# Two-layer attention encoder on one core: output banks drained one step later, B's output blocks summed in pairs, dense work respread

## The chip, the cores and the metric

The kernel runs on one core of one Trainium2 chip, in one launch. The metric is the device time of that launch in microseconds. The engines are TensorE (PE; its weight loads PEld overlap its matmuls), VectorE (DVE), ScalarE (ACT), GpSimd (POOL) and SyncE (SP, which issues the DMAs). They run their own instruction streams and meet only at semaphores.

## What is computed

An encoder of two layers on x (1 × 1024 × 1024, float32). Each layer is a norm, an input projection, attention by heads, a gate and an output projection, then a norm and a residual sum. Layer 0 has two kinds of heads side by side: A, differential attention (4 heads, two softmaxes each, all earlier keys), and B, a sliding window (8 query heads, 2 heads of keys and values, one chunk of 64 back, with learned sinks). Layer 1 has C, 16 heads over a band of nine chunks with a learned relative bias.

```python
D_MODEL = 1024; SEQ = 1024; DEPTH = 2; CHUNK = 64; HEAD_DIM = 64
A_HEADS = 4; B_HEADS = 8; B_KV_HEADS = 2; B_PREV_CHUNKS = 1; C_HEADS = 16; C_PREV_CHUNKS = 8
# A, per head: two softmaxes
s = jnp.where(allowed, s - slopes[None, :, None, None, None] * dist, NEG)
p = jax.nn.softmax(s, axis=-1)
a = p[:, :, 0] - lam * p[:, :, 1]
o = rms_norm(einsum('bhqk,bkhe->bqhe', a, v), subln_g) * (1.0 - lam_init)
# B, per head: band of two chunks, a sink in the softmax
p = jax.nn.softmax(jnp.concatenate([s, sink], axis=-1), axis=-1)[..., :-1]
# C, per head: band of nine chunks, learned bias
p = jax.nn.softmax(jnp.where(valid, q @ k * scale + bias, NEG), axis=-1)
# each layer: every branch times its gate g * sigmoid(g), output projection, then
x = x + rms_norm(concat(branches * silu(gates)) @ w_out, post_norm_g)
```

## The kernel before, in words

**Precision.** Every float32 operand of a product is split into a rounded part and a rest (hi and lo, type fp32r), and each product is three matmuls: hi·hi, hi·lo, lo·hi. The weights are split by POOL (`split`, L799 and L802), everything else by ACT (hi) and DVE (lo).

**Tiling.** A tile is 128 rows or columns. A unit is two heads (A: one head with its two softmaxes): A0 to A3, B0 to B7 (each half of the sequence of a pair of heads), C0 to C7. A unit of A or C has 16 items, one for each tile of 128 queries of a head, in 20 steps; a B unit has 8 items in 8 steps. Units start at steps 0, 20, 40, 60 (A), 80 to 136 by 8 (B), then 8 steps of bridge between the layers, C0 at 152, C1 at 172 and so on; 322 steps in all.

**The steps.** A planner in Python lays the whole program out in steps. Each engine walks the steps in the same order, and its stream is fixed by the code of that walk:

- PE in step s: an early use of the output bank (only when the step has two or more), the input products of the step (`project`, L926, 128×512 each, 24 to a fill of a bank), a late use of the output bank, product of the probabilities with v (`times_v`, L1004), transposes of probabilities (`turn`, L1048), scores (`score`, L1078), then further late uses, the last outputs and transposes of v.
- ACT: the hi part of transposed probabilities (L1205), exp (L1176), the hi parts of fills, and so on.
- DVE in iteration s: `lo_of_turned` (L1474) and `lowest` (L1410: scores plus bias and their minimum) of step s−1; `normalise` (L1420, L1424; for A also L1429, L1432) of step s−2, for the units that are not deferred (A and C1 to C6); `denominators` (L1449) of step s−2 for the deferred ones (B, C0, C7), which are normalised after the product with v by `times_rec` (L1458); the gate; the lo parts of fills; and the uses of the output bank of step s; `out_sum` (L1482).

**Banks.** Input fills go to dense banks 0 and 1 in turn. All uses of the output bank, number 2, are called spare uses: output products (three matmuls L933 for one head pair, 128 rows and 512 columns, that DVE adds into y: L1387, for A L1379 and L1381 with the norm's factor, for C0 a copy L1385), row transposes of the norm between the layers (L960), and A's sums of squares (L954). PE may write the bank again when DVE has read it (`bank_free[2]`). Output products of unit i run during unit i+1: for A and C one use per step in 16 of the steps 3 to 19. B's run two per step in steps 13 to 16 from the start of their unit; A3's in steps 3 to 8 of B0, C6's in steps 3 to 8 of C7.

**lowest** of step s−1 waits for the semaphore `scored`, which the last scores matmul of the step raises, and PE's later scores wait for `lowest` in turn (`low_done`).

Of the kernel before, what the change touches and what calls it, by code (L numbers as in the profile page):

```python
# [13 lines left out]
P = 128  # L14
# [25 lines left out]
class Unit:  # L40
# [35 lines left out]

    def order(self):
# [13 lines left out]
C = [Unit("C", i, 80 + 64 + BRIDGE + 20 * i) for i in range(8)]  # L91
# [3 lines left out]
TOTAL = C[7].start + 30  # L95
# [59 lines left out]
class Fill:  # L155
# [7 lines left out]
    hi: int = 0  # L163


@dataclass(eq=False)
class Spare:
# [3 lines left out]
    u: Unit = None  # L171
    row: int = 0
    half: int = 0
    block: object = None
# [24 lines left out]
for u_ in UNITS:  # L199
    for j_, (h_, t_) in enumerate(u_.order()):  # L200
        k0_ = {"A": 0, "B": max(0, t_ - 1), "C": max(0, t_ - 4)}[u_.kind]
        it_ = Item(u_, h_, t_, len(ITEMS), u_.start + j_, k0_, t_ + 1 - k0_)
# [18 lines left out]
        if u_.kind != "A" or h_ == 1:  # L221
            g_ = Turned("p", u_, -1, it_.step + 3, item=it_, first=ITEMS[-2] if u_.kind == "A" else it_)
            GROUPS.append(g_)
            it_.group = len(GROUPS) - 1
            if t_ % 2:
                pv_ = Pv(u_, h_, t_ - 1, len(PVS), g_.step + 1, g_)
# [23 lines left out]
V_TURNS += [Turned("v", C[i], 6 + i, C[i - 1].start + 19) for i in range(1, 8)]  # L250
# [56 lines left out]
for i_ in range(8):  # L307
    f_ = B[i_].half
    segment([("g", B[i_], f_)] + ([("q", B[i_ + 1], B[i_ + 1].half)] if i_ < 7 else []), B[i_].start, B[i_].start + 7)
segment([("q", C[0], 0), ("k", C[0], 0), ("v", C[0], 0), ("g", C[0], 0)], C[0].start - BRIDGE, C[0].start - 1)  # L310
segment([("q", C[0], 1), ("k", C[0], 1)], C[0].start + 8, C[0].start + 8)
segment([("v", C[0], 1)], C[0].start + 9, C[0].start + 10)
segment([("g", C[0], 1)] + both("v", C[1]), C[0].start + 11, C[0].start + 15)
for i_ in range(7):
    if i_:
        segment(both("g", C[i_]) + both("v", C[i_ + 1]), C[i_].start, C[i_].start + 15)
    if i_ < 6:
        segment(both("k", C[i_ + 1]) + both("q", C[i_ + 1]), C[i_].start + 16, C[i_].start + 19)
segment([("k", C[7], 0), ("q", C[7], 0)], C[6].start + 16, C[6].start + 19)
segment([("k", C[7], 1), ("q", C[7], 1), ("g", C[7], 0), ("g", C[7], 1)], C[7].start, C[7].start + 7)  # L320
# [1328 lines left out]
```

## Time and profile before

| | us |
|---|---|
| median of 3 runs (lowest, highest) | 1391.14 (1386.51, 1396.16) |
| the profiled execution | 1392.36 |
| its span, from first to last instruction | 1390.4 |
| PE busy in it | 1234.1 (89%) |
| DVE busy | 891.2 (64%) |
| ACT busy | 580.6 (42%) |
| POOL busy | 389.3 (28%) |

The mean granted TensorE clock of the profiled execution was 0.952 of full speed. The steps stand in the trace at: A1 to A3 131 to 358 us, B0 to B4 358 to 520, B5 to B7 520 to 638, bridge 638 to 675, C0 675 to 800, C1 to C6 800 to 1260, C7 and the end from 1260 on. A busy time counts the instructions of an engine on one clock; matmuls overlap each other in the records, so the distance of two starts is the time that a matmul takes from PE, not its recorded length. "A <- B" in the waits is an idle time of A that ended when B finished.

### The profile page before, as it was taken

To read this page: it belongs to the slowest core of one execution; us is meant where nothing else is said; L and a number is where in the kernel's file an instruction comes from. 1 tells how busy PE (TensorE), PEld (TensorE's weight loads), DVE (VectorE), ACT (ScalarE), POOL (GpSimd) and SP (SyncE) were. 2 spreads that over 40 slices of the span, in tenths; PEclk is the share of its full clock that TensorE was granted. 3 is DMA by queue.
4 is the path that set the end of the run, shared out by engine and by line. 5 is a ranking of instruction groups with operands and counts; after the bars stand their busy time and mean duration, and the time that the engine had idled before them with its cause. 6 is when DMAs were issued, how large, how long until landed. Compare 5 with 4: busy or idle time off the path is not lost.

```text
span 1390.4 us, 17337 instructions
## 1 busy us (share of the span) xinstructions
PE 1234.1 (89%) x6480; PEld 1043.0 (75%) x6480; DVE 891.2 (64%) x1789; ACT 580.6 (42%) x1271; POOL 389.3 (28%) x280
## 2 busy tenths in 40 slices
PE   6999999999878877768568999999999999998863
PEld 6978888888766665656457888888888888886652
DVE  5575857677576676765444386766847586675667
ACT  5544434434333434433333444444444354443332
POOL 4322131231423334433722212213230222312002
PEclk9999999999999999889779999999999999999976
DMA  6341020110211122222211111102110211111302
GB/s 197 107 127 61 16 62 16 35 42 16 62 46 46 48 78 91 91 76 61 91 61 46 51 46 50 46 16 65 31 65 16 65 31 50 46 35 31 121 31 91
DMA packets 86243, 82.07 MB, mean 59 GB/s; under 512 B 3184, under 2 KB 74864, under 8 KB 86160
## 3 DMA queue, kind: packets, MB, share of 16 engines
q1 hardware_dynamic: 86160, 80.97, 18.6%
q8 instruction: 51, 0.84, 0.3%
q14 instruction: 32, 0.26, 0.1%
HBM read 72.52 MB, written 13.68 MB: 62 GB/s over the span
## 4 chain that ended last, share of the span: by engine, by line
PE 74%; DVE 13%; ACT 5%; issue 4%; POOL 2%; DMA 1%; SPq 0%; POOLq 0%; DVEq 0%; ACTq 0%
PE dense L926 38%; PE dense L933 13%; PE pv_ps L1004 8%; PE scores L1078 6%; PE turned L1048 5%; PE dense L901 3%; DVE e_sb L1410 2%; DVE y L1387 2%; DVE rec_wide L1449 1%; DVE pT_lo L1474 1%; ACT e_sb L1176 1%; DVE yT_lo L1530 1%; PE dense L960 1%; ACT pT_hi L1205 1%; PE turned L1036 1%
## 5 line engine op out<-in xcount | busy, mean ns | idle before, releaser
L926 PE MATMUL dense<-hT_hi,w_hi 128*128 128x512 f32 x880 | 354.8, 403 | 0.0
L926 PE MATMUL dense<-hT_lo,w_hi 128*128 128x512 f32 x880 | 348.5, 396 | 0.0
L926 PE MATMUL dense<-hT_hi,w_lo 128*128 128x512 f32 x880 | 347.9, 395 | 0.0
L1176 ACT ACTIVATE e_sb<-e_sb,low 128x256 f32<-128x256 f32 (+7 forms) x256 | 170.7, 667 | 371.3 <-DVE low L1410 371.3
L799 POOL TENSOR_SCALAR w_hi<-w_f 128x1024 fp32r<-128x1024 f32 x90 | 102.0, 1133 | 793.2 <-PE dense L926 663.7
L802 POOL TENSOR_TENSOR w_lo<-w_f,w_hi 128x1024 fp32r<-128x1024 f32 x90 | 219.7, 2441 | 7.5
L926 PEld LDWEIGHTS dense<-hT_hi,w_lo 128*128 128x128 f32 x880 | 167.8, 191 | 37.7
L926 PEld LDWEIGHTS dense<-hT_lo,w_hi 128*128 128x128 f32 x880 | 168.6, 192 | 28.9
L926 PEld LDWEIGHTS dense<-hT_hi,w_hi 128*128 128x128 f32 x880 | 168.4, 191 | 29.2
L1474 DVE TENSOR_TENSOR pT_lo<-turned,pT_hi 128x640 fp32r<-128x640 f32 (+3 forms) x224 | 133.7, 597 | 55.7 <-ACT pT_hi L1205 52.7
L933 PE MATMUL dense<-w_hi,yT_hi 128*128 128x512 f32 x256 | 111.0, 434 | 62.6 <-DVE y L1387 43.6
L1004 PE MATMUL pv_ps<-pT_hi,v_st 128*128 128x256 f32 x536 | 133.3, 296 | 27.6 <-DVE pT_lo L1474 27.6
L1387 DVE TENSOR_TENSOR y<-dense,y 128x512 f32<-128x512 f32 x160 | 110.1, 688 | 64.3 <-PE dense L933 63.1
L1205 ACT ACTIVATE pT_hi<-turned 128x640 fp32r<-128x640 f32 (+3 forms) x224 | 117.1, 523 | 63.1 <-PE turned L1048 60.7
L1078 PE MATMUL scores<-k_hh,q_st 128*128 128x384 f32 (+3 forms) x352 | 130.4, 370 | 4.9 <-DVE k_l L1357 3.5
L1410 DVE CUSTOM_DVE_ANT_0 e_sb<-scores,bias 128x640 f32<-128x640 f32 (+3 forms) x192 | 130.9, 682 | 4.2 <-PE scores L1078 2.8
L1048 PE MATMUL turned<-ident,e_sb 128*128 128x128 f32 x744 | 121.8, 279 | 8.0 <-DVE pT_lo L1474 6.5
L1004 PEld LDWEIGHTS pv_ps<-pT_hi,v_st 128*128 128x128 f32 x536 | 101.5, 198 | 36.0 <-DVE pT_lo L1474 32.3
L1004 PE MATMUL pv_ps<-pT_lo,v_st 128*128 128x256 f32 x456 | 122.2, 292 | 0.0
L933 PEld LDWEIGHTS dense<-w_hi,yT_hi 128*128 128x128 f32 x256 | 50.5, 197 | 91.0 <-DVE y L1387 56.3
L1048 PEld LDWEIGHTS turned<-ident,e_sb 128*128 128x128 f32 x744 | 93.6, 143 | 25.3 <-DVE pT_lo L1474 7.4
L1078 PE MATMUL scores<-k_l,q_st 128*128 128x384 f32 (+3 forms) x352 | 111.4, 325 | 0.0
(128 smaller groups left out, 1789.5 us busy)
## 6 DMA issues: line engine op xcount, KB each, us to landing
w_f<-in_w_in_c SPq DMA_DIRECT2D x36, 512.0 KB, 4.0
w_f<-in_w_in_ab SPq DMA_DIRECT2D x34, 512.0 KB, 3.9
w_f<-in_w_out_ab SPq DMA_DIRECT2D x12, 512.0 KB, 3.6
rel_tiles_dram<-rel_rows_dram SPq DMA_DIRECT2D x1, 5120.0 KB, 23.1
bias<-rel_tiles_dram SPq DMA_DIRECT2D x8, 640.0 KB, 5.3
y<-in_x SPq DMA_DIRECT2D x8, 512.0 KB, 7.7
xs<-in_x SPq DMA_DIRECT2D x8, 512.0 KB, 3.6
x_dram<-y SPq DMA_DIRECT2D x8, 512.0 KB, 4.1
```

The source lines that it names most:

```text
L799: ts(hi, src, 1.0, 1.0, ALU.mult, ALU.mult).then_inc(w_hi_done, 1)
L802: tt(w_lo[:, slot, :], src, hi, ALU.subtract).then_inc(w_ready, 1)
L926: last = mm(dense[:, x.n % 2, :], lhs[:, d * P:(d + 1) * P], rhs[:, d, x.f * HALF:(x.f + 1) * HALF], start=i == 0, stop=i == 23)
L933: last = mm(bank, lhs[:, cols], rhs, start=n == 0, stop=n == 2)
L1004: last = mm(pv_ps[:, p.n % 2, :], v_st[:, which, kt, :], p_part[:, kt - p.t + 6, :], start=i == 0 and m == 0, stop=i == p.count - 1 and m ...
L1048: last = nc.tensor.transpose(turned[:, at0:at0 + P], e_sb[:, e0:e0 + P], ident[:])
L1078: last = mm(scores[:, at0:at0 + w], q_st[:, it.h, c:c + P], k_part[:, kh, key:key + w], start=i == 0, stop=i == 1)
L1176: copy(e, e, ACT.Exp, scale=-1.0, bias=stat_col(low, it.j), accum_out=stat_col(total, it.j)).then_inc(s_exp, 1)
L1205: copy(pT_hi[:, r, q], turned_tile(x), ACT.Copy).then_inc(s_thi, 1)
L1387: last = tt(into, dense[:, 2, :], into, ALU.add)
L1410: nc.vector.tensor_tensor_reduce(out=e_of(it), in0=scores[:, it.off:it.off + it.n * P], in1=bias_of(it), scale=-u.slope(it.h), scalar=star ...
L1474: tt(pT_lo[:, r, q], turned_tile(x), pT_hi[:, r, q], ALU.subtract).then_inc(s_tlo, 1)
```

## The change

1. **DVE drains the output bank an iteration later.** The uses of step s are read in iteration s+1 (all but an early one), and in an iteration `lowest` now comes first, then `lo_of_turned`, `normalise`, `denominators`, and only then the bank. Fills are drained one iteration later too, except in the last four steps of a unit of A or C (at the end of the same iteration). `out_sum`, `times_rec` and ACT's `out_low` move one step later. Further late uses behind the scores are gone from PE's step.
2. **B's outputs in pairs.** `out_matmuls` sums the blocks of two units B in one bank (six matmuls, one add into y instead of two). The weights of the second block need a place of their own, in vT (hi) and in the space of C's bias (lo, with a fourth and fifth load slot). The uses are spread, one per step, over steps 3 to 12 of the unit behind the pair and the next; A3's over steps 3 to 13 of B0 (one and two in turn).
3. **A narrow reciprocal.** The reciprocal of the deferred units is taken of four columns on DVE and widened to 128×256 by an ACT copy (`widen`), where it was taken of 128×256 on DVE.
4. **Deferred units turn their probabilities one step earlier** (two steps behind the scores), and for B there is a second set of columns of pT.
5. **Dense work is respread**: C0's later items one step later, C1 and all behind it one step later; the q of C0 is projected in B7, the v of C1 and C7 partly in steps 0 to 5 of C0 and C7, C7's k, q and g over its steps 0 to 9; C6's outputs are one per step over 16 steps of C7; the last outputs use two banks and come a step earlier. The program has 320 steps.

```diff
         for s in range(TOTAL):
+            for it in ITEMS_AT.get(s - 1, []):
+                lowest(it)
             for x in TURNED_AT[s - 1]:
                 lo_of_turned(x)
-            for it in ITEMS_AT.get(s - 1, []):
-                lowest(it)
             for it in ITEMS_AT.get(s - 2, []):
                 if not it.u.deferred:
                     normalise(it)
-            for r, it, _ in recs_at(s, 2):
+            for r, it in DENOMINATORS_AT[s]:
                 denominators(r, it)
...
+            for x in LATE_AT.get(s - 1, []) + EARLY_AT[s]:
+                spare_use(x)
+            for _, n, row, half, _ in LAST_AT.get(s - 1, []):
+                last_out(n, row, half)
+            for x in FILLS_AT[s]:
+                if not x.tail:
+                    lo_of_fill(x)
             for g in GATES_AT[s]:
                 gated(g)
+            for p in PVS_AT.get(s - 1, []):
+                out_sum(p)
+            for r, p in RECS_AT[s - 1]:
+                times_rec(r, p)
             for g in GATES_AT.get(s - 1, []):
                 gated_lo(g)
-            uses = SPARES_AT.get(s, [])
-            early = uses[:-1][:1]
-            for x in early:
-                spare_use(x)
...
-            for x in uses[len(early):]:
-                spare_use(x)
-            for _, n, row, half, _ in LAST_AT[s]:
-                last_out(n, row, half)
-            for p in PVS_AT[s]:
-                out_sum(p)
-            for r, it, p in recs_at(s, 5):
-                times_rec(r, it, p)
```

The pairs, their plan, the reciprocal and its copy:

```diff
-        def out_matmuls(bank, cols, w, w_l):
-            for n, (lhs, rhs) in enumerate(((yT_hi, w), (yT_hi, w_l), (yT_lo, w))):
-                last = mm(bank, lhs[:, cols], rhs, start=n == 0, stop=n == 2)
+        def out_matmuls(bank, parts):
+            for m, (c, w, w_l) in enumerate(parts):
+                for n, (lhs, rhs) in enumerate(((yT_hi, w), (yT_hi, w_l), (yT_lo, w))):
+                    last = mm(bank, lhs[:, c:c + P], rhs, start=m == n == 0, stop=m == len(parts) - 1 and n == 2)
...
-b0_ = B[0].start
-out_steps(A[3], [(b0_ + 3, 3), (b0_ + 4, 3), (b0_ + 5, 3), (b0_ + 6, 3), (b0_ + 7, 2), (b0_ + 8, 2)])
-for i_ in range(7):
-    s_ = B[i_].start + 13
-    out_steps(B[i_], [(s_, 2), (s_ + 1, 2), (s_ + 2, 2), (s_ + 3, 2)])
+out_steps((A[3],), [(B[0].start + 3 + t, 1 + t % 2) for t in range(11)])
+for i_ in range(0, 6, 2):
+    s_ = B[i_ + 1].start + 8
+    out_steps((B[i_], B[i_ + 1]), [(s_ + t, 1) for t in (3, 4, 6, 7, 8, 9, 11, 12)])
...
-out_steps(C[6], [(s_ + 3, 3), (s_ + 4, 3), (s_ + 5, 3), (s_ + 6, 3), (s_ + 7, 2), (s_ + 8, 2)])
+out_steps((C[6],), [(s_ + 4 + t, 1) for t in range(16)], (2, 3, 4, 5, 6, 7, 0, 1))
...
-            nc.vector.reciprocal(rec_wide[:].rearrange("p (o h a) -> p h o a", o=2, h=2),
-                                 src.rearrange("p (h o a) -> p h o a", h=2, a=1).broadcast_to([P, 2, 2, HD])).then_inc(s_drec, 1)
+            nc.vector.reciprocal(stat_col(rec, it.j - 3, 4), src).then_inc(s_drec, 1)
```

DVE in a step of C before, in a unit that is not deferred: `pT_lo` is the lo part of the transposed probabilities, the ISA rows are `lowest`, `y` the add of the output bank.

```order
L1474 TENSOR_TENSOR pT_lo<-turned,pT_hi 128x5x128 [waits turned_hi]
L1410 ISA e_sb,low<-scores,bias 128x640 [waits turned_done,scored]
L1410 ISA low 128x1
L1420 RECIPROCAL rec<-total 128x1 [waits exp_done]
L1424 TENSOR_SCALAR e_sb<-e_sb,rec 128x640 [waits rec_done]
L1387 TENSOR_TENSOR y<-dense,y 128x512 [waits spare_filled]
L1482 TENSOR_TENSOR o_sb<-pv_ps,o_sb 64x256 [waits pv_low]
```

And in the same step after:

```order
L1485 ISA e_sb,low<-scores,bias 128x640 [waits turned_done,scored]
L1485 ISA low 128x1
L1546 TENSOR_TENSOR pT_lo<-turned,pT_hi 128x5x128 [waits turned_hi]
L1495 RECIPROCAL rec<-total 128x1 [waits exp_done]
L1499 TENSOR_SCALAR e_sb<-e_sb,rec 128x640 [waits rec_done]
L1462 TENSOR_TENSOR y<-dense,y 128x512 [waits spare_filled]
L1554 TENSOR_TENSOR o_sb<-pv_ps,o_sb 64x256 [waits pv_low]
```

The two ISA rows have moved ahead of `pT_lo`. The y add stands at the same distance from them as before, but it is now that of the step whose scores these ISA rows wait for; before it was that of the next step.

PE in the same step after (its rows are in the same order before), L992 being the input products, L1000 the output products:

```order
L992 MATMUL dense<-hT_lo,w_hi 128x512
L992 MATMUL dense<-hT_hi,w_lo 128x512
L1000 MATMUL dense<-w_hi,yT_hi 128x512 [waits bank_free2]
L1000 MATMUL dense<-w_lo,yT_hi 128x512
L1000 MATMUL dense<-w_hi,yT_lo 128x512
L1111 MATMUL turned<-ident,e_sb 128x128 [waits probs,turned_lo]
L1111 MATMUL turned<-ident,e_sb 128x128 x4
L1141 MATMUL scores<-k_hh,q_st 128x384 [waits low_done]
L1141 MATMUL scores<-k_l_57,q_st 128x384
L1141 MATMUL scores<-k_hh,q_st 128x256
```

The output products wait for `bank_free2`, which the y add raises, behind the input products of their step.

DVE in B before, where output products stand two to a step and the wide reciprocal is at its place:

```order
L1410 ISA e_sb,low<-scores,bias_b,sinks 128x256 [waits turned_done,scored]
L1410 ISA low 128x1
L1387 TENSOR_TENSOR y<-dense,y 128x512 [waits spare_filled] x2
L1458 TENSOR_TENSOR o_sb<-o_sb,pv_ps 128x256 [waits out_bc,rec_turned]
L1474 TENSOR_TENSOR pT_lo<-turned,pT_hi 128x2x128 [waits turned_hi]
L1410 ISA e_sb,low<-scores,bias_b,sinks 128x128 [waits turned_done,scored]
L1410 ISA low 128x1
L1443 TENSOR_TENSOR den<-total,sink_e 128x4 [waits sink_e,exp_done]
L1449 RECIPROCAL rec_wide<-den 128x2x2x64 [waits den_pair]
L1524 SCALAR_TENSOR_TENSOR o_sb<-o_sb,gate 128x256 [waits bank_free1,rec_times]
```

And after:

```order
L1485 ISA e_sb,low<-scores,bias_b,sinks 128x128 [waits turned_done,scored]
L1485 ISA low 128x1
L1546 TENSOR_TENSOR pT_lo<-turned,pT_hi 128x2x128 [waits turned_hi]
L1518 TENSOR_TENSOR den<-total,sink_e 128x4 [waits sink_e,exp_done]
L1522 RECIPROCAL rec<-den 128x4 [waits den_pair]
L1462 TENSOR_TENSOR y<-dense,y 128x512 [waits spare_filled]
L1596 SCALAR_TENSOR_TENSOR o_sb<-o_sb,gate 128x256 [waits bank_free1,rec_times]
L1485 ISA e_sb,low<-scores,bias_b,sinks 128x256 [waits turned_done,scored]
L1485 ISA low 128x1
```

One y add stands where two did, and the reciprocal has four columns.

## Rows read from the trace of the kernel before

**Rows 1.** The page: its head and section 1
```profile
span 1390.4 us, 17337 instructions
...
PE 1234.1 (89%) x6480; PEld 1043.0 (75%) x6480; DVE 891.2 (64%) x1789; ACT 580.6 (42%) x1271; POOL 389.3 (28%) x280
```

**Rows 2.** Windows: from:to and length (us), busy (x instructions), PEclk, DMA share, GB/s
```profile
131.00:358.00 227.00, 226.89 (x1197) 193.56 (x1197) 160.79 (x304) 96.90 (x187) 57.72 (x32) 1.00 0.13 40
358.00:520.00 162.00, 131.26 (x658) 105.80 (x657) 110.13 (x239) 60.06 (x179) 53.55 (x35) 0.97 0.17 50
520.00:638.00 118.00, 87.03 (x400) 68.53 (x399) 77.16 (x159) 47.68 (x131) 44.45 (x38) 0.86 0.25 77
638.00:675.00 37.00, 32.08 (x153) 25.81 (x152) 18.78 (x34) 11.75 (x26) 21.11 (x15) 1.00 0.28 79
675.00:718.00 43.00, 18.92 (x74) 14.55 (x73) 22.60 (x40) 17.30 (x41) 21.85 (x19) 0.61 0.28 90
718.00:800.00 82.00, 77.46 (x403) 66.23 (x402) 32.21 (x54) 31.02 (x58) 23.00 (x16) 0.96 0.16 48
800.00:1260.00 460.00, 459.79 (x2520) 396.73 (x2519) 311.65 (x699) 210.70 (x438) 100.05 (x68) 1.00 0.14 43
1260.00:1390.40 130.40, 85.41 (x388) 68.82 (x386) 81.86 (x132) 41.71 (x87) 21.01 (x21) 0.83 0.18 69
```

**Rows 3.** Waits in 358:638: who, for whom: us in total, times, longest
```profile
PE dense L933 <- DVE y L1387: 31.6, 23, 3.6
```

**Rows 4.** Timeline, a step of C1: start us, us, engine, line, operation
```profile
915.74 0.28 PE L1078 MATMUL scores<-k_l,q_st 128*128 128x256 f32 x1
...
915.85 0.40 PE L926 MATMUL dense<-hT_hi,w_hi 128*128 128x512 f32 x1
...
916.20 0.82 DVE L1474 TENSOR_TENSOR pT_lo<-turned,pT_hi 128x640 fp32r<-128x640 f32 x1 [0.38 <-ACT pT_hi L1205]
...
916.94 0.82 DVE L1410 CUSTOM_DVE_ANT_0 e_sb<-scores,bias 128x640 f32<-128x640 f32 x1
...
917.22 0.39 PE L933 MATMUL dense<-w_hi,yT_hi 128*128 128x512 f32 x1
...
917.68 0.16 DVE L1420 RECIPROCAL rec<-total 128x1 f32<-128x1 f32 x1
...
917.88 0.56 DVE L1424 TENSOR_SCALAR e_sb<-e_sb,rec 128x640 f32<-128x640 f32 x1
...
918.35 0.68 DVE L1387 TENSOR_TENSOR y<-dense,y 128x512 f32<-128x512 f32 x1
```

**Rows 5.** Timeline, DVE in a step of A2
```profile
245.82 1.08 DVE L1410 CUSTOM_DVE_ANT_0 e_sb<-scores,bias 128x896 f32<-128x896 f32 x1
...
247.02 0.68 DVE L1429 TENSOR_SCALAR e_sb<-e_sb,rec,neg_lam 128x768 f32<-128x768 f32 x1
247.74 1.02 DVE L1432 SCALAR_TENSOR_TENSOR e_sb<-e_sb,rec 128x768 f32<-128x768 f32 x1
248.67 0.75 DVE L1381 SCALAR_TENSOR_TENSOR y<-dense,rms,y 128x512 f32<-128x512 f32 x1
```

**Rows 6.** Timeline, PE's wait for the y add in a B step
```profile
511.30 0.68 DVE L1387 TENSOR_TENSOR y<-dense,y 128x512 f32<-128x512 f32 x1
...
512.04 0.50 PE L933 MATMUL dense<-w_hi,yT_hi 128*128 128x512 f32 x1 [0.48 <-DVE y L1387]
...
512.38 0.40 PE L933 MATMUL dense<-w_lo,yT_hi 128*128 128x512 f32 x1
```

**Rows 7.** Lines by form, DVE in 358:638: group | busy us, mean ns | idle before
```profile
L1449 DVE RECIPROCAL rec_wide<-den 128x256 f32<-128x256 f32 x15 | 26.3, 1753 | 0.5
L1410 DVE CUSTOM_DVE_ANT_0 e_sb<-scores,bias_b,sinks 128x256 f32<-128x256 f32 x55 | 26.1, 475 | 0.2 <-PE scores L1078 0.2
L1474 DVE TENSOR_TENSOR pT_lo<-turned,pT_hi 128x256 fp32r<-128x256 f32 x52 | 21.9, 421 | 9.6 <-ACT pT_hi L1205 9.0
```

**Rows 8.** Lines by form, DVE in 131:358
```profile
L1432 DVE SCALAR_TENSOR_TENSOR e_sb<-e_sb,rec 128x896 f32<-128x896 f32 x3 | 9.5, 3174 | 0.1
```

More of the change, by code:

```diff
@@ L75, in place, with step, in_tail @@
         return slice(f * HALF, (f + 1) * HALF)
+    def step(self, j):
+        return self.start + j + (1 if self.kind == "C" and self.i == 0 and j >= 8 else 0)
+    def in_tail(self, s):
+        return self.kind != "B" and s >= self.step(16)
     def order(self):
@@ L94 @@
     u_.n = n_
[L95 removed]
+TOTAL = C[7].start + 27
 @dataclass(eq=False)
@@ L163 @@
     hi: int = 0
+    tail: bool = False
+    drain: int = 0
 @dataclass(eq=False)
@@ L170 @@
     use: int
-    u: Unit = None
+    units: tuple = ()
     row: int = 0
     half: int = 0
-    block: object = None
+    blocks: tuple = ()
 @dataclass(eq=False)
@@ L326, with out_steps @@
     f_.hi = sum(1 for o_ in FILLS[:f_.n] if o_.b != "v")
+    f_.tail = any(u_.in_tail(f_.step) and f_.step < u_.step(20) for u_ in UNITS if u_ is not C[7])
+    f_.drain = f_.step if f_.tail else f_.step + 1
 FILL_OF = {(f_.b, f_.u, f_.f): f_ for f_ in FILLS}
 SPARE_RAW = []
-def out_steps(u, plan):
-    rows = range(4 * u.half, 4 * u.half + 4) if u.kind == "B" else range(ST)
+def out_steps(units, plan, rows=None):
+    if rows is None:
+        rows = range(4 * units[0].half, 4 * units[0].half + 4) if units[0].kind == "B" else range(ST)
     fills = [(row, half) for row in rows for half in range(2)]
@@ L338, in out_steps @@
         for row, half in fills[n:n + count]:
-            SPARE_RAW.append((step, "out", u, row, half))
+            SPARE_RAW.append((step, "out", units, row, half))
         n += count
-    assert n == len(fills), (u, n)
+    assert n == len(fills), (units, n)
 def even_plan(first, n, steps):
@@ L430, in freed @@
             return ("pro", PRO_DONE[b], 0)
+    if blocks[n].u is B[1]:
+        return ("spare", SUM_OF[A[3]].use + 1, B[0].start + 1)
+    if blocks[n].u is B[7]:
+        return ("fill", FILL_OF["g", B[7], 1].n + 1, FILL_OF["g", B[7], 1].step)
     return None
@@ L479, in final_rows, with gate_of @@
     return [(n, row) for a, n, row in FINAL if a + lag == s]
+def gate_of(u, row):
+    c = u.col(row)
+    return max(g.n for g in GATES if g.u is u and same_columns(g.cols, slice(c, c + P)))
 def previous_gate(u, cols):
@@ L747, in _ @@
             for w in LOADS_AT.get(s, []):
+                if w.u is B[1] and w.b == "o":
+                    if new(s_low, 64):
+                        sp.wait_ge(s_low, 64)
                 freed_by(w.slot_free)
```

284 lines of the change are left out of this document (160 added, 124 removed).

## The prediction

> **What bounds the kernel now.** I read the page's head first, then the table of windows, because the head mixes stages with different limits. PE is busy for 1234.1 of 1390.4 us and DVE for 891.2 [rows 1]. By windows there are two kinds of stage [rows 2]. In A1 to A3 (131 to 358) and C1 to C6 (800 to 1260) PE is busy for 226.89 of 227 us and for 459.79 of 460 at clock 1.00: there its own matmuls set the time, half of the kernel. In B0 to B7 and the bridge (358 to 675) it is busy for 131.3 + 87.0 + 32.1 = 250.4 of 317 us, and the clock falls to 0.97 and 0.86. At the entry of layer 1 (675 to 718) and in the tail (1260 on) it waits too. In B the largest waits of PE are for the output bank: 31.6 us in 23 waits for the y add L1387 [rows 3].
>
> **Where the new loop is.** All output products use one bank, and the y add on DVE frees it. Before, DVE adds the use of step s in iteration s, ahead of anything that needs the scores of s. After, it adds the use of step s in iteration s+1, behind lowest(s), which waits for the last matmul of step s; lo_of_turned(s), the reciprocal and normalise stand ahead of it too. PE reaches the output products of s+1 after only the six input products. So from the last scores of step s two paths run to the next output products, and the longer one sets the time.
>
> PE's own path: the six input products take from 915.85 to 917.22, 1.37 us or 0.23 each [rows 4].
> DVE's path, for a C step of five key tiles [rows 4]: the last scores matmul is issued at 915.74 and runs 0.28, so it ends 0.17 after PE's next issue at 915.85; lowest takes 0.74 (916.94 to 917.68), lo_of_turned 0.74 (916.20 to 916.94), reciprocal 0.20 (917.68 to 917.88), normalise 0.47 (917.88 to 918.35), the add 0.68. For the end of the add to PE's restart, a wait in B shows 511.30 + 0.68 = 511.98 to 512.04, and 0.34 instead of 0.23 to the next product [rows 6]: 0.06 + 0.11. With 0.02 to DVE's start that is 0.36 + 0.74 + 0.74 + 0.20 + 0.47 + 0.68 = 3.19 us, so PE waits 3.19 − 1.37 = **1.82 us in every such step**.
>
> **C1 to C6.** The first output use has nothing to wait for. Then each unit has one step of about 0.64 (less normalising), and the steps up to 15 sum to 17.3 us with the shorter tiles of the first rows; 0.5 is added for DVE instructions slowed while POOL writes. The last four steps have 24 input products, 24 × 0.23 = 5.5 us, ahead of the output products and hide it all. That gives 17.8 us per unit, 89 for C1 to C5. C6 has only 4.5 products of cover per step (36 over 16 steps less; 12 waits × 1.5 × 0.23 = 4.1 more) and loses 24 products to C7 (5.4): 17.8 + 4.1 − 6 (rounded with one out use gone) = 16. **C: +105.** Reordering lo and lowest by itself costs nothing: PE waits for neither by the rows.
>
> **A1 to A3.** The chain is longer. At 7 tiles lowest is 1.08 against 0.82 at 5 [rows 4, 5], at 6 tiles the two normalise instructions take 0.72 and 0.93 (247.02 to 248.67), the add 0.75 [rows 5]. Per tile I take 0.13 for lowest and, alike, for lo_of_turned, and 0.2 for the pair (an estimate from these). Odd steps (a turned group and two normalised heads) wait 1.49 to 3.82, mean 2.65, six of them: 15.9; even steps have no lo_of_turned and wait 0.30 to 0.96: 3.8. Where POOL is splitting weights the second normalise takes 3174 ns at 896 columns [rows 8] against 1.02 us at 768 [rows 5]: about 2.3 per unit reaches the loop now that DVE is on PE's path. 22 us per unit. **A: +66.**
>
> **B and the bridge.** The pairs put two heads' blocks in one bank: 32 fewer adds of 0.69 on DVE (22 us), the products of PE stay. The wide reciprocal, 1753 ns [rows 7], becomes one of four columns (0.16, as the reciprocal of one column in rows 4) and a copy on ACT, which is busy for 108 of 280 us there [rows 2]: 15 × 1.6 = 24 us of DVE freed in B. DVE was busy for 187 of 280, so PE no longer waits for it to catch up. The same loop bounds what is gained, without normalise: 0.36 + 0.40 (lowest, 0.475 less overlap) + 0.34 (lo_of_turned, 0.421 likewise) + 0.69 = 1.79 against 1.37, 0.42 per step, 3.4 per unit of eight steps. PE's work by the pitch of its matmuls (0.23, 0.12 and 0.11) is 22.5 to 25 per unit. B0 to B4 become 137 (from 162), B5 to B7, where row norms and a lower clock add 16, become 100 (from 118) and the bridge 32 (from 37). **B: −48.** Bounds: all waits for L1387 stay but for the adds saved (−20); all of 66.6 idle and the clock loss of some 21 come back, and A3's outs spread well (−100 with the bridge at its work).
>
> **Entry of layer 1.** A step of C0 is put in, but a fill of C0's q is made in B7 already, and 718 to 800 loses 6 us of products that stand elsewhere now (its v of C1 in the first steps, where PE is busy for 18.9 of 43). The chain of 675 to 718, whose clock is 0.61, stays. **−7**, bounds 0 and −15.
>
> **Tail.** PE is busy for 85.4 and DVE for 81.9 of 130.4. Four wide reciprocals less 1.6 each, the last outputs a step earlier and the 24 products of C6 (+5.4, in idle time) against the C6 outputs spread one per step: **−16**, bounds 0 and −35.
>
> **Other edits.** Waits of the additional weight slots and the later loads of C's bias fall on SP and POOL, whose splits wait for PE in most cases; I take them as free (if a split came late a fill would wait a few us; that lies in the range). The ACT reordering puts exp ahead of the fills, with ACT at 43 to 46% in A and C: nothing.
>
> **Sum** against the profiled execution's own 1392.4 (span 1390.4 and 2.0 around it): + 66 + 105 − 48 − 7 − 16 = 1492. The profiled one stands 1.2 above the median, so **1491 us**.
>
> A rule that speaks against the change. The trace shows one output bank that cost nothing in A and C, 0.2 us of 460 [rows 2], as long as its add came early. The Trainium skill (Perfetto Trace Analysis, Optimizing Tensor Performance (Matmuls)) wants independent matmul groups to rotate through different PSUM banks so that the evacuation of one overlaps the next group. By that rule alone only the add itself would be exposed, 0.68 us in 12 steps of 9 units, 73 us, where the rows give 171: what is queued ahead of the evacuation counts for more than the evacuation.
>
> **The rivals.**
> 1. *The loop and the clock as well* (0.14). In B0 to B4, where PE is idle for 19% of the time in short waits, the granted clock was 0.97, and 0.86 in B5 to B7 at 26% [rows 2]. A and C would be idle for 19 to 22%, in waits of under 4 us. At 0.97 over the 860 us of these stages as they become that is +26: 1517. Against it: the waits are short, with 3 to 6 us of full work between.
> The Trainium skill (TensorE: Matmul & The Clock Gate, A second HAM failure mode: psum-queue depth-cycling) describes just such micro-idling between matmul groups that makes the clock oscillate; no row of before in A or C shows it.
> 2. *A smaller loop* (0.10). If PE's end, the restart and the collisions overlap, A and C cost 133 instead of 171, and B and the tail may give 15 more: about 1440.
> 3. *A wash* (0.04): the loop at its lower bound, 133, and the gains near their upper ones, 133 of 100 + 15 + 35: 1391.
> 4. *Faster* (0.04): the add is hidden in A and C after all, because DVE reaches it inside PE's cover. It decides where the chain is under 1.37 us; the add and lowest alone are 1.42, so it needs DVE not to wait for the step's last scores. Then only the gains are left: 1391 − 71 = 1320. For it speaks that DVE is busy for only 68% of 800 to 1260.
> The forecast itself has 0.68.
>
> **The numbers.** The forecast's own range is 1455 to 1525 (the loop 150 to 193 with the gains between 50 and 90); rival 1 lies in it. With rival 2's edge the range is **1440 to 1530**, some 0.82. What a measurement of this kernel can tell from no change is about 1%. Faster by over 1%: 0.05 (rival 4 and part of 3); within 1%: 0.03; slower: 0.92.
>
> **What would show it.** In the profile after: waits of PE's output products L1000 for the y adds L1462 of about 1.8 us in nearly every step of C1 to C6, some 12 per unit, and PE's busy share of 100% down to about 80%; a C unit of 96 us (78.5 before), an A unit of 98 (76 before). DVE idle ahead of lowest L1485 for PE's scores, where now it comes to scores that are long done. The 15 wide reciprocals of B gone, a B unit of 26 us for 31. The clock at 1.00 in A and C (rival 1: under 0.98). I am wrong if A1 to A3 and C1 to C6 keep their 227 and 460 us, or if those waits stay under 1 us.

## The result, and the profile after

The changed kernel takes 1547.38 us, median of 4 runs (1544.52 to 1549.66), against 1390.82 for the kernel before measured beside it: 1.112 times as long, 95% interval 1.108 to 1.117. The forecast was 1491 with a range to 1530: the direction was right, the size too small by 56 us, a third of the slowdown of 157.

The profiled execution has a span of 1542.6 us. Its page, head and section 1, in the form of [rows 1]:

```profile
span 1542.6 us, 17427 instructions
...
PE 1275.5 (83%) x6480; PEld 1045.7 (68%) x6480; DVE 830.5 (54%) x1758; ACT 588.6 (38%) x1296; POOL 395.5 (26%) x286
```

DVE does 61 us less than before and waits more. PE has the same 6480 matmuls and is busy for 41 us more: some of them ran at half clock, and the record of the first matmul behind a wait is longer (C1 has no half clock, and PE is busy for 81.8 us in it against 78.9 without the waits, in the run with the add in its own step everywhere). The windows over the stages, to be read beside [rows 2] (A1 to A3; B0 to the bridge; the entry of layer 1 with the rest of C0; C1 to C6; the tail; columns as there):

```profile
129.30:442.20 312.90, 256.92 (x1204) 208.95 (x1202) 162.40 (x304) 96.00 (x187) 58.25 (x33) 0.91 0.10 29
442.20:715.70 273.50, 234.42 (x1194) 188.56 (x1192) 160.09 (x399) 127.22 (x353) 119.51 (x89) 0.96 0.24 74
715.70:847.60 131.90, 98.64 (x485) 81.35 (x485) 48.12 (x93) 47.66 (x101) 45.64 (x36) 0.87 0.19 61
847.60:1424.20 576.60, 483.53 (x2496) 393.92 (x2493) 309.18 (x698) 211.04 (x437) 100.87 (x70) 0.98 0.11 35
1424.20:1542.60 118.40, 88.42 (x410) 72.84 (x408) 75.45 (x133) 43.74 (x93) 23.88 (x23) 0.84 0.21 80
```

| stage | before, us | after, us | difference | forecast |
|---|---|---|---|---|
| ahead of A1 | 131.0 | 129.3 | −2 | 0 |
| A1 to A3 | 227 | 312.9 | +86 | +66 |
| B0 to the bridge | 317 | 273.5 | −43 | −48 |
| C0 | 125 | 131.9 | +7 | −7 |
| C1 to C6 | 460 | 576.6 | +117 | +105 |
| tail | 130.4 | 118.4 | −12 | −16 |

In the two stages that were PE's own, PE is now busy for 82% and 84%. DVE and ACT do the same work in them as before; they only wait longer. The waits of the stretch of C1 to C6 (who, for whom: us in total, times, longest):

```profile
DVE e_sb L1485 <- PE scores L1141: 169.9, 78, 5.2
...
PE dense L1000 <- DVE y L1462: 74.0, 61, 2.1
...
PE dense L1000 <- DVE y L1460: 14.3, 12, 2.1
...
PE dense L1000 <- DVE yT_lo L1602: 4.7, 6, 1.9
```

The first and the second row are the two halves of a loop: DVE waits for PE's scores, then PE waits for DVE's add. 73 waits for the two forms of the add stand in the trace, and six, one per unit, for the lo part of the gated output (L1602). Their mean is 1.2 us, less than the 1.82 of the forecast, since steps with shorter tiles wait less and a row counts 0.28 us less than the wait costs (shown with a step below).

### The profile page after: what moved, and what is told of

The parts are those of the page before. It is cut to its first block, busy times and chain, and to the rows that moved or that the text cites. A ratio compares the mean times of both kernels' runs of the same rounds, so it can differ in the third digit from the quotient of the medians.

```text
span 1542.6 us, 17427 instructions
## 1 busy us (share of the span) xinstructions
PE 1275.5 (83%) x6480; PEld 1045.7 (68%) x6480; DVE 830.5 (54%) x1758; ACT 588.6 (38%) x1296; POOL 395.5 (26%) x286
## 4 chain that ended last, share of the span: by engine, by line
PE 58%; DVE 27%; issue 3%; ACT 3%; POOL 1%; DMA 1%; DVEq 0%; POOLq 0%; ACTq 0%
PE dense L992 22%; PE dense L1000 14%; PE pv_ps L1067 8%; PE scores L1141 6%; DVE e_sb L1485 6%; PE turned L1111 5%; DVE pT_lo L1546 5%; DVE y L1462 3%; DVE e_sb L1499 3%; DVE e_sb L1507 2%; DVE y L1456 1%; DVE e_sb L1504 1%; DVE q_st L1425 1%; PE dense L1026 1%; PE turned L1099 1%
## 5 line engine op out<-in xcount | busy, mean ns | idle before, releaser
L992 PE MATMUL dense<-hT_hi,w_hi 128*128 128x512 f32 x880 | 357.1, 406 | 7.3 <-DVE k_l L1431 4.4
L992 PE MATMUL dense<-hT_lo,w_hi 128*128 128x512 f32 x880 | 349.8, 397 | 0.0
L992 PE MATMUL dense<-hT_hi,w_lo 128*128 128x512 f32 x880 | 349.3, 397 | 0.0
L864 POOL TENSOR_SCALAR w_hi<-w_f 128x1024 fp32r<-128x1024 f32 x88 | 96.6, 1098 | 955.9 <-PE dense L992 846.2
L1000 PE MATMUL dense<-w_hi,yT_hi 128*128 128x512 f32 x224 | 109.1, 487 | 187.5 <-DVE y L1462 93.1
L1000 PEld LDWEIGHTS dense<-w_hi,yT_hi 128*128 128x128 f32 x224 | 43.5, 194 | 256.3 <-DVE y L1462 131.3
L867 POOL TENSOR_TENSOR w_lo<-w_f,w_hi 128x1024 fp32r<-128x1024 f32 x88 | 215.0, 2443 | 7.3
L992 PEld LDWEIGHTS dense<-hT_hi,w_hi 128*128 128x128 f32 x880 | 169.6, 193 | 36.1 <-issue 8.2
L992 PEld LDWEIGHTS dense<-hT_hi,w_lo 128*128 128x128 f32 x880 | 168.6, 192 | 37.6
L992 PEld LDWEIGHTS dense<-hT_lo,w_hi 128*128 128x128 f32 x880 | 169.8, 193 | 27.2
L1067 PE MATMUL pv_ps<-pT_hi,v_st 128*128 128x256 f32 x536 | 141.7, 310 | 3.5 <-DVE pT_lo L1546 2.9
L1067 PE MATMUL pv_ps<-pT_lo,v_st 128*128 128x256 f32 x456 | 126.5, 301 | 0.0
L1067 PEld LDWEIGHTS pv_ps<-pT_hi,v_st 128*128 128x128 f32 x536 | 109.1, 214 | 10.0 <-DVE pT_lo L1546 5.1
L1111 PEld LDWEIGHTS turned<-ident,e_sb 128*128 128x128 f32 x744 | 94.2, 144 | 20.2 <-DVE pT_lo L1546 1.9
L1067 PEld LDWEIGHTS pv_ps<-pT_lo,v_st 128*128 128x128 f32 x456 | 96.0, 211 | 4.0
```

Source lines behind the costliest of these rows:

```text
L864: ts(hi, src, 1.0, 1.0, ALU.mult, ALU.mult).then_inc(w_hi_done, 1)
L867: tt(lo_place(slot), src, hi, ALU.subtract).then_inc(w_ready, 1)
L992: last = mm(dense[:, x.n % 2, :], lhs[:, d * P:(d + 1) * P], rhs[:, d, x.f * HALF:(x.f + 1) * HALF], start=i == 0, stop=i == 23)
L1000: last = mm(bank, lhs[:, c:c + P], rhs, start=m == n == 0, stop=m == len(parts) - 1 and n == 2)
L1067: last = mm(pv_ps[:, p.n % 2, :], v_st[:, which, kt, :], p_part[:, kt - p.t + 6 - pT_set(p), :], start=i == 0 and m == 0, stop=i == p.coun ...
L1111: last = nc.tensor.transpose(turned[:, at0:at0 + P], e_sb[:, e0:e0 + P], ident[:])
```

## The experiments

Each run is compared with the kernel before on the same chip; the stages are cut in each trace at the first products of their first step, 1.4 to 4.2 us ahead of its first scores. Stages and waits are those of the profiled execution, times and ratios those of the medians.

### The add made in its own step again, in A and C alone

```diff
+OWN = set(range(A[1].start, A[3].start + 20)) | set(range(C[1].start, C[7].start))
+DRAIN_AT = {s: ([] if s - 1 in OWN else LATE_AT.get(s - 1, [])) + EARLY_AT[s] + (LATE_AT[s] if s in OWN else []) for s in range(TOTAL)}
...
-            for x in LATE_AT.get(s - 1, []) + EARLY_AT[s]:
+            for x in DRAIN_AT[s]:
                 spare_use(x)
```

> The changed kernel, in which DVE again adds the output bank's use of step s in iteration s (at the same place of the iteration) in A1 to A3 and C1 to C6 alone; everything else stays, lowest ahead of lo_of_turned too. If the late add is the loop that costs the time, A1 to A3 fall from 312.9 us back to about 227 and C1 to C6 from 576.6 to about 455 (24 products fewer than before), PE is busy for over 99% there at clock 1.00, and the time is about 1547 - 86 - 121 = 1340 us. If the time went into something else of the change (lowest ahead of lo_of_turned, fills and out_sum read a step later, the turned groups), these stages keep most of their length and the time stays above 1500.

It took 1351.44 us (1350.42 to 1352.86), 0.970 of the kernel before (0.967 to 0.973), 196 us less than the changed kernel. The windows of A1 to A3 and of C1 to C6:

```profile
130.80:363.40 232.60, 229.44 (x1203) 193.55 (x1201) 159.57 (x304) 94.42 (x187) 59.22 (x33) 1.00 0.13 39
...
769.60:1234.40 464.80, 458.51 (x2494) 391.78 (x2493) 314.63 (x698) 211.35 (x438) 102.54 (x69) 1.00 0.14 43
```

80 and 112 us are back, PE is busy for 98.6% at clock 1.00. What is left over 227 and 455 is 6 and 10 us; an experiment below takes 3 of it, and the rest stays open. So the place of one DVE instruction per step is worth 192 us here, and without it the rest of the change is a gain of 3%.

### The same in every step

The edit is the one above with OWN set to all steps; ACT's part of the row transposes moves along.

> The same edit in every step of the program, B, C0 and C7 as well (ACT's part of the row transposes moves along). If the loop costs B about 0.4 us in each of its steps with an output, and C0's row transposes go through the same bank, it is 10 to 25 us below the run that edits A and C alone: 1315 to 1330. If B, C0 and C7 are held by other things (the chain through exp, denominators and the gate), it is within 5 us of that run; if DVE now waits for PE's later output products and holds up its chain, it is above it.

1335.18 us (1331.29 to 1336.82), 0.958 of before (0.955 to 0.961). B with the bridge goes from 272.6 to 268.0 us, the first eight steps of C0 from 50.4 to 42.7. PE's waits in those eight steps, of the run above and then of this one:

```profile
PE dense L1028 <- DVE hT_lo L1441: 13.7, 4, 8.2
...
PE dense L1028 <- DVE xs L1676: 8.0, 2, 6.7
```

```profile
PE dense L1028 <- DVE xs L1676: 8.3, 3, 4.1
...
PE dense L1028 <- DVE hT_lo L1441: 3.4, 2, 1.9
```

The row transposes use the output bank as well, and DVE's `hT_lo` frees it: the loop stood there too, 8.2 us long at its worst, since ahead of the second read stood what waits for the scores.

### The late add kept, PE's output products behind its scores

```diff
+            if s not in OWN:
+                for x in LATE_AT[s]:
+                    spare_use(x)
...
                 score(it)
+            if s in OWN:
+                for x in LATE_AT[s]:
+                    spare_use(x)
```

> The changed kernel with DVE's late add kept, but in A1 to A3 and C1 to C6 PE makes the output products of a step behind its scores instead of behind its input products. The add of step s-1 then has a whole PE step of cover (2.6 to 5 us) instead of the six input products' 1.37. If it is the short cover that makes the loop, A1 to A3 and C1 to C6 are back at about 227 and 455 us and the time is 1340, as with the early add. If the late add is bad by itself (DVE busier, or its clock effects), the time stays well above that.

1368.51 us (1367.78 to 1371.38), 0.983 of before (0.980 to 0.986). C1 to C6 take 464 us, as with the early add: a whole step covers a chain of 3.2 us, late add or not. A1 to A3 take 248, 15 more than with the early add, so 1340 was too low. PE still waits for the y add there, 15.7 us in twelve waits, four in each unit (0.9, 1.6, 2.0 and up to 1.1 us). They stand in the later steps of the unit, where DVE's chain is longest. It is the cover against the chain that decides, in both directions.

### The late add alone, in the kernel before

```diff
                 denominators(r, it)
             if s == 1:
                 constants()
+            if s - 1 in OWN:
+                for x in SPARES_AT.get(s - 1, []):
+                    spare_use(x)
...
             early = uses[:-1][:1]
+            if s in OWN:
+                uses, early = [], []
```

> The kernel before with one part of the change: in A1 to A3 and C1 to C6 the add of step s's output bank is made in iteration s+1, behind lo_of_turned, lowest, normalise and denominators. Nothing of B, C0 and C7 is touched. If this alone makes the loop, A1 to A3 take about 313 us instead of 227 and C1 to C6 about 575 instead of 460, and the time is about 1391 + 86 + 113 = 1590 us, slower than the whole change. If the loop needs the other parts as well, it stays below 1450.

1597.13 us (1593.85 to 1601.78), 1.147 of before (1.143 to 1.151). Windows of A1 to A3 and C1 to C6:

```profile
128.80:441.80 313.00, 257.65 (x1204) 210.78 (x1202) 161.84 (x304) 97.36 (x187) 58.27 (x34) 0.91 0.10 29
888.00:1467.50 579.50, 486.68 (x2524) 396.96 (x2521) 308.59 (x700) 211.47 (x438) 99.73 (x69) 0.99 0.11 34
```

The stages are those of the whole change within 3 us (C6 has its 24 products more here). The late add is enough by itself; no other part of the change is needed for the loop.

### The late add directly behind lowest

```diff
                 lowest(it)
+            if s - 1 in OWN:
+                for x in LATE_AT[s - 1]:
+                    spare_use(x)
             for x in TURNED_AT[s - 1]:
                 lo_of_turned(x)
```

> The changed kernel with the late add kept (step s in iteration s+1) in A1 to A3 and C1 to C6, but directly behind lowest, so that lo_of_turned, the reciprocal and normalise no longer stand ahead of it. By the sum of the chain a C step of five tiles waits 0.36 + 0.74 + 0.68 - 1.37 = 0.41 us instead of 1.85, an A step of n tiles 0.13n - 0.18 instead of up to 3.8, and the clock has no cause left to fall in A. That is 250 us for A1 to A3 (312.9), 491 for C1 to C6 (576.6) and a time of about 1398. If the time of the loop is not the sum of what stands ahead of the add, but a fixed cost of waiting for the scores, it stays above 1480.

1400.22 us (1395.8 to 1404.14, 10 runs), 1.005 of before (1.004 to 1.007). Windows of A1 to A3 and C1 to C6:

```profile
129.50:385.60 256.10, 237.55 (x1204) 192.93 (x1202) 164.81 (x304) 95.99 (x187) 55.83 (x33) 0.99 0.12 36
787.50:1275.60 488.10, 472.12 (x2496) 384.68 (x2493) 311.15 (x698) 211.16 (x437) 101.34 (x70) 1.00 0.13 41
```

That is 256 and 488, against 250 and 491 from the sum of the chain. The add still waits for the step's last scores, yet 147 us are back: the wait is the sum of what stands between the scores and the add, and lo_of_turned, the reciprocal and normalise were most of it.

### lo_of_turned ahead of lowest again, late add kept

```diff
+            for x in TURNED_AT[s - 1]:
+                lo_of_turned(x)
             for it in ITEMS_AT.get(s - 1, []):
                 lowest(it)
-            for x in TURNED_AT[s - 1]:
-                lo_of_turned(x)
```

> The changed kernel with the old order of two DVE operations alone: lo_of_turned ahead of lowest again, the late add kept. lo_of_turned needs only the transposes, which PE makes ahead of the scores, and takes 0.74 us at 5 tiles. If all that stands ahead of the add counts wherever it stands, the loop keeps its length and the time stays at 1547 within 10 us. If what counts is only the part of the chain behind the scores, lo_of_turned partly runs while PE makes the scores (0.6 us at 5 tiles), the wait of 1.85 us shrinks by 0.3 to 0.6 in each step with a turned group, and the time is 1500 to 1530.

1573.2 us (1571.74 to 1575.78), 1.130 of before (1.127 to 1.133): 26 us slower than the changed kernel, outside both expectations. In A nothing moves (313), in C1 to C6 5 us. B and the bridge take 290 us against 273.5, 17 of the 31 between the two profiled executions. DVE's waits for ACT in B and the bridge, of the changed kernel and then of this one:

```profile
DVE pT_lo L1546 <- ACT pT_hi L1265: 3.4, 5, 0.9
```

```profile
DVE pT_lo L1546 <- ACT pT_hi L1265: 74.8, 40, 3.3
```

`lo_of_turned` waits for ACT's hi part, which ends later than the scores in B. With it first, lowest stands behind ACT's copy, and exp behind lowest. With lowest first, ACT's copy is hidden behind it. DVE's waits for the scores there fall from 63.1 to 1.2 us in return, so DVE itself waits only some 10 us more; but ACT's waits for `lowest`, ahead of exp, rise from 39.0 to 72.3 us. So this half of the reordering is a gain in B, which the prediction had put at nothing. That exp carries it to PE is argued from the order, not tested. In C the loop keeps its length for the same reason: in a step of C1 the hi part ends at 903.33 in the changed kernel, 0.15 us behind the last scores, so lo_of_turned can't run while PE makes the scores, as the second expectation had it.

### PE's waits in A filled with matmuls on zeros

```diff
+WAIT_FILL = {5: 4, 7: 8, 9: 8, 11: 10, 12: 2, 13: 12, 15: 21}
...
+                for _ in range(WAIT_FILL[j]):
+                    mm(dense[:, f.n % 2, :], zeros[:], hT_hi[:, 0, 0:HALF], start=False, stop=False)
```

> The changed kernel with PE's waits in A1 to A3 filled: in the steps where PE waits for the y add it makes 4 to 21 more matmuls of 128x512 whose stationary tile is zero (they add nothing to the bank), 2 to 21 of them per step, 0.9 to 4.8 us, a little less than each measured wait (1.2 to 5.5 us). PE then does not sit idle. The granted clock was 0.87 in A1's steps with waits (129 to 206), and matmuls behind the long waits stood 0.43 us apart instead of 0.23. If the rest of A's miss, some 9 us per unit over the forecast, is the clock that falls in the waits, A1 to A3 fall from 312.9 us to about 288 at clock 1.00 and the time to about 1522 us. If the clock's fall hides inside the waits and the miss is chain length, nothing comes back: 1547 or some us more.

1523.0 us (1521.06 to 1524.85), 1.093 of before (1.091 to 1.096): 195 more matmuls, and 24 us less than the changed kernel. The stretch of A1 to A3 is 293 us long, at clock 1.00:

```profile
129.30:422.00 292.70, 282.04 (x1406) 229.34 (x1404) 154.56 (x304) 96.06 (x187) 58.07 (x34) 1.00 0.11 32
```

A1 to A3 end 20.2 us earlier than in the changed kernel: 293 is the stage's length with the loop and a full clock, and the other 20 us were the clock. The changed kernel's trace shows how. PE in step 15 of A1 (the wait for the add, then the products with v), and windows of the same stretch:

```profile
194.36 0.39 PE L992 MATMUL dense<-hT_hi,w_lo 128*128 128x512 f32 x1
200.25 0.80 PE L1000 MATMUL dense<-w_hi,yT_hi 128*128 128x512 f32 x1 [5.49 <-DVE y L1454]
200.84 0.63 PE L1000 MATMUL dense<-w_lo,yT_hi 128*128 128x512 f32 x1
201.27 0.63 PE L1000 MATMUL dense<-w_hi,yT_lo 128*128 128x512 f32 x1
```

```profile
194.00:196.00 2.00, 0.75 (x4) 0.29 (x2) 1.96 (x5) 1.24 (x2) 1.07 (x2) 1.00 0.03 9
196.00:198.00 2.00, 0.00 (x0) 0.00 (x0) 1.97 (x2) 0.00 (x0) 2.00 (x1) 0.71 0.87 248
198.00:200.00 2.00, 0.00 (x0) 0.00 (x0) 2.00 (x2) 0.00 (x0) 0.58 (x1) 0.50 0.02 5
200.00:202.00 2.00, 1.75 (x5) 1.47 (x6) 0.19 (x1) 0.00 (x0) 0.00 (x0) 0.50 0.00 0
```

While PE stands still the granted clock falls from 1.00 to 0.50 (2.4 to 1.2 GHz), in the window from 196 to 198, and it is still there when the wait is over: products of 512 columns follow each other every 0.43 us (200.84 to 201.27) instead of 0.23. A wait need not be that long. In A1 to A3 the rows show fifteen waits of 2.1 us or more, and the clock fell to 0.50 in or within 1 us behind thirteen of them. In C1 to C6, where most waits are shorter and the longest is 2.1, it fell six times, each time behind a wait of 1.9 to 2.1 us, and others of that length left it alone. C1 has no such fall and C2 has one:

```profile
847.60:944.30 96.70, 81.78 (x431) 66.68 (x429) 52.26 (x118) 36.01 (x74) 18.02 (x13) 1.00 0.13 41
944.30:1042.50 98.20, 83.30 (x431) 68.28 (x430) 52.04 (x118) 35.81 (x74) 18.09 (x13) 0.98 0.11 34
```

C2 is 1.5 us longer with the same work, and C3, again without a fall, takes 96.7 us. At 1.5 us each the six falls cost C1 to C6 some 9 us (an estimate from these units; no run fills C's waits).

### The wide reciprocal put back, and the pairs undone

Both start from the kernel with the add in its own step everywhere (1335).

```diff
-            nc.vector.reciprocal(stat_col(rec, it.j - 3, 4), src).then_inc(s_drec, 1)
+            if new(s_rturn, r):
+                dve.wait_ge(s_rturn, r)
+            nc.vector.reciprocal(rec_wide[:].rearrange("p (o h a) -> p h o a", o=2, h=2),
+                                 src.rearrange("p (h o a) -> p h o a", h=2, a=1).broadcast_to([P, 2, 2, HD])).then_inc(s_drec, 1)
```

> Against the run with the early add in every step (1335): the wide reciprocal on DVE is put back (128x256, 1.75 us, no copy on ACT), all else kept. If DVE's 1.6 us more stand on a path to PE in B, C0 and C7 (24 of them), B grows from 268 us by 10 to 20 and the time is 1348 to 1362. If the reciprocal lay beside PE's work, the time stays at 1335 and the gain in B comes from the pairs and the spread.

1349.47 us (1349.03 to 1350.19): 14.3 us more, 12 of them in B and the bridge (279.9 against 268.0). DVE was freed of 24 × 1.6 = 38 us by it, so a good third of that reached the time. (ACT loses its copy of 0.41 us in return.)

```diff
         for row, half in fills[n:n + count]:
-            SPARE_RAW.append((step, "out", units, row, half))
+            for u in units:
+                SPARE_RAW.append((step, "out", (u,), row, half))
```

> Against the run with the early add in every step (1335): B's blocks are no longer summed in pairs in the bank; each of the two is a use of its own with its own add of 0.69 us, 32 adds more on DVE, in the same steps, PE's products unchanged. If the adds of DVE bound B, it is 10 to 25 us slower: 1345 to 1360. If DVE has room for them now that the reciprocal is narrow, the time is within 5 us of 1335.

1357.16 us (1353.95 to 1360.95): 22 us more, with 32 adds of 0.69 us more on DVE, 19 of them in B and the bridge. Here each added microsecond of DVE cost one of the kernel. The range of both: 0.969 (0.966 to 0.971) and 0.974 (0.971 to 0.978) of before.

### Two more waits taken away

```diff
-    f_.tail = any(u_.in_tail(f_.step) and f_.step < u_.step(20) for u_ in UNITS if u_ is not C[7])
+    f_.tail = f_.b in "kq" or any(u_.in_tail(f_.step) and f_.step < u_.step(20) for u_ in UNITS if u_ is not C[7])
...
+            for g in GATES_AT[s]:
+                if whole(g):
+                    gated(g)
+            for g in GATES_AT.get(s - 1, []):
+                if whole(g):
+                    gated_lo(g)
             for x in DRAIN_AT[s]:
                 spare_use(x)
```

> The run with the early add in every step, with two more waits of its trace taken away: k and q fills are read by ACT and DVE at the end of their own iteration (they were read one later, and the first scores of each B unit waited 2.3 to 2.9 us for q), and the whole-unit gates of A and C1 to C6 are computed ahead of the bank's adds (the first output product of 9 units waited 1.0 us for them). If these waits are ended by what the trace names, 7 x 2.4 + 9 x 0.9 = 25 us come back: 1310 us. If something else comes last there (exp, the v fills), less than 10 us come back.

1312.73 us (1311.28 to 1313.69), 0.942 of before (0.940 to 0.944), 22 us below the run that it starts from. B and the bridge fall from 268.0 to 255.5:

```profile
360.70:616.20 255.50, 227.65 (x1196) 188.26 (x1194) 160.66 (x399) 125.57 (x352) 119.40 (x89) 0.97 0.25 78
```

C0's second part falls from 82.9 to 74.2: PE no longer waits for `k_l` there, and the clock is 1.00 where it was 0.94, which takes the other 4.3 us off PE's busy time. The wait in the run that it starts from, in 673 to 756:

```profile
PE dense L994 <- DVE k_l L1433: 4.4, 1, 4.4
```

A1 to A3 gain 3 us, the earlier gates' part; C1 to C6 gain nothing (464.7), so there the first output product is held by something that comes last with the gate and that these runs don't name. This kernel beats both: it is 80 us below the kernel before, measured beside it.

Two further steps from it brought nothing. lo_of_turned ahead of lowest:

> The run with early add, own-iteration k and q fills and earlier gates (1313), with lo_of_turned ahead of lowest again. In its trace PE's product with v waits 0.5 us for pT_lo in 2 to 3 steps of each unit of A and C, since lowest (up to 1.15 us) stands ahead of it. If the order costs that, 8 to 12 us come back: 1303. If the scores then wait for lowest instead, nothing changes.

1322.31 us (1322.01 to 1323.57), 10 us slower. A and C gain 3 us, B with the bridge loses 12: the same finding as above, without the loop.

The first four row transposes one step later (`a_ + (6 if r_ < 4 else 5)`):

> The run with early add, own-iteration k and q fills and earlier gates (1313), with the row transposes of the first four rows of layer 1 one step later, in B5 and B6. PE waited 6.3 us there for the normed row (xs) in two steps, and the clock fell behind it. If one step of 3 to 5 us covers it, 5 to 10 us come back: 1305. If the norm's own chain (POOL and ACT between DVE's parts) only gets later with it, nothing changes.

1311.22 us (1309.73 to 1313.32), the same within the measurement. B5 to the bridge take 131 us in both. PE no longer waits there for the normed row (`xs`, 1.3 us, against 10.7 in the kernel that the run starts from), but for `hT_lo` instead (8.3 us in four waits).

## Why the prediction was right or wrong

**What bounds the kernel** and **where the new loop is**: right. The late add alone makes the loop (1597), its removal alone ends it (1351).

**The chain of 3.19 us and the wait of 1.82**: right to a few hundredths. A step of C1's second half in the changed kernel, PE and DVE, beside [rows 4, 6]:

```profile
903.02 0.39 PE L992 MATMUL dense<-hT_hi,w_hi 128*128 128x512 f32 x1
...
903.22 0.82 DVE L1485 CUSTOM_DVE_ANT_0 e_sb<-scores,bias 128x640 f32<-128x640 f32 x1 [3.63 <-PE scores L1141]
...
903.97 0.82 DVE L1546 TENSOR_TENSOR pT_lo<-turned,pT_hi 128x640 fp32r<-128x640 f32 x1
...
904.70 0.15 DVE L1495 RECIPROCAL rec<-total 128x1 f32<-128x1 f32 x1
904.89 0.55 DVE L1499 TENSOR_SCALAR e_sb<-e_sb,rec 128x640 f32<-128x640 f32 x1
905.36 0.68 DVE L1460 COPY y<-dense 128x512 f32<-128x512 f32 x1
...
906.10 0.50 PE L1000 MATMUL dense<-w_hi,yT_hi 128*128 128x512 f32 x1 [1.53 <-DVE y L1460]
```

From the first input product to the output product 3.08 us instead of 1.37, and 0.11 more to the next one: 1.82. The row's own idle time, 1.53, is shorter because the modelled end of the last input product lies 0.17 behind the moment at which PE could issue the next one; that and the 0.11 are the 0.28 us by which a row understates a wait.

**C1 to C6: +105, measured +117.** Two things were left out. "The first output use has nothing to wait for" was wrong: it waited for `yT_lo`, by the rows 0.6 us in each of five units and 1.9 in C6, since the gate now stands behind the bank and the fills in DVE's iteration. And the clock, put at 1.00, fell six times, some 9 us, three of the falls in C6, which lost 21 us instead of 16 at a mean clock of 0.94. The loop itself was priced right: C1, with no fall, takes 96.7 us and 79.7 with the add in its own step, 17.0 against the 17.8 of the forecast.

**A1 to A3: +66, measured +86. This is the step that failed.** The clock was left out of the sum ("The clock at 1.00 in A and C") and priced only in rival 1, at 3% over both A and C with a chance of 0.14, against which the text put that "the waits are short, with 3 to 6 us of full work between". In A the waits of steps 7 to 15 were 2.1 to 5.5 us, the clock was 0.91, and 20 us were lost: with PE kept busy the stage is 293 us long, +66. With C's 9 us the clock makes some 29 of the 53 us by which the stages together miss. The prediction had priced the waits of A itself (up to 3.82, and 2.3 more for POOL) and still called them all "under 4 us" and short.

That the length without the clock is +66 to the microsecond is part luck. 6 of the 66 are there with the add in its own step too (232.6 against 227), which the sum has no term for; the loop alone is 60.

**POOL's collision** (2.3 us per unit): near. The second normalise at 896 columns takes 3.11 us in each unit, in the chain of step 15, where its neighbours suggest about 1.15 (an estimate, halfway between 1.02 at 768 and 1.29 at 1024 columns): 2.0 us more.

**B: −48, measured −43.** The parts were right in kind: in B the pairs are worth 19 us, the narrow reciprocal 12, and the loop that stays costs 5 (272.6 against 268.0). What was missing is that two effects of other edits nearly cancel: lowest ahead of lo_of_turned is worth 17, and reading q a step later costs some 12 (with the add in its own step everywhere the first scores of the units waited 17.0 us for q, in seven waits). These five add up to 31 of the 43; they were measured from different kernels, and what the spread of the outputs is worth was not tested.

**C0: −7, measured +7. Wrong in its step** that the chain of 675 to 718 stays: it grew from 43.0 to 50.0 us. The prediction looked for the loop where PE was full and not where the same bank carries row transposes: 7.7 us by the run with the add in its own step everywhere, which has the chain at 42.7. Another 8.7 are the late read of k, a wait of 4.4 us and the clock behind it. The fills' later reading has no term in the prediction; "Other edits" names only ACT's new order, and puts it at nothing.

**Tail: −16, measured −12**: the loop again; with the add in its own step everywhere the tail is 4 us shorter (114.6).

**The rule on banks.** By the first experiment the loop in A and C is worth 192 us, some 163 without the clock's 29; the prediction had 171 from the rows. The Trainium skill's rule on rotating PSUM banks (Perfetto Trace Analysis, Optimizing Tensor Performance (Matmuls)) would have given 73: it names the right resource, but an evacuation of 0.68 to 0.75 us made a wait of up to 5.5 through what stood ahead of it in its queue. On the clock the trace agrees with the Trainium skill (TensorE: Matmul & The Clock Gate, A second HAM failure mode: psum-queue depth-cycling), which has the clock go to and fro when PE idles briefly between groups of matmuls: thirteen falls in A, six in C.

**The rivals.** 1 came, and its price of 26 us for A and C together is near the 29 measured, but two thirds of it fell on A (its sign, a clock under 0.98, shows there alone), and its 1517 leaves 30 us to C0, to B, to the tail and to C's first output uses. 2, 3 and 4 did not come; rival 4's condition, that the add doesn't wait for the step's scores, is just what the first two experiments made, and they gave 1351 and 1335 where rival 4 said 1320.

## What to carry to other kernels

When the reading of a bank moves later in its engine's queue, list what it now stands behind, mark what of that waits for the writer's own latest work, and compare the sum with the work that the writer has until it needs the bank: the wait is the difference, in every round. Do this for every user of the bank, not only where it is used most. Then look at each wait's length, and price the matmul clock as a term of its own: in this kernel waits of 2.1 to 5.5 us in A cost 20 us by the clock on top of the 60 of the loop, and C's, mostly under 2, some 9 on top of 103. If such waits can't be removed, filling them can pay; here it gave back 24 us.

## What was not expected of the hardware

- Useless work made the kernel faster: 195 matmuls on a zero tile, some 45 us of PE time in waits, brought 1547 to 1523 us, by a clock that stayed at 1.00 where it had been 0.91.
- The clock fell to 1.2 GHz at thirteen of the fifteen waits of 2.1 us or more in A, and at six of some 79 in C, which are 2.1 us or shorter (clock 1.00 in C1, 0.98 in C2).
- DVE's scalar_tensor_tensor of 128x896 took 3.11 us in the changed kernel where its neighbours of 768 and 1024 columns took 1.02 and 1.29. It began at 196.42; POOL's tensor_tensor ran from 195.97 to 198.58, and DVE ended 0.95 us behind it, at 199.53:

```profile
195.97 2.61 POOL L867 TENSOR_TENSOR w_lo<-w_f,w_hi 128x1024 fp32r<-128x1024 f32 x1
```

```profile
196.42 3.11 DVE L1507 SCALAR_TENSOR_TENSOR e_sb<-e_sb,rec 128x896 f32<-128x896 f32 x1
```

It did not run beside POOL's instruction but behind it. The Trainium skill (SBUF — State Buffer, SBUF: two separate sides) describes the port pair that DVE and GpSimd share as an exclusive lock held for a whole instruction; the trace agrees for this pair of instructions.
